# Two products of 256 columns merged into one of 512 in the feed-forward ups of a two-block transformer kernel

## The reference, cut to what matters

```
def causal_dwconv(x, w):            # y[t] = sum_k w[k] x[t-K+1+k], K = 3 here
def conv_ffn(h, w_up, conv_w, w_down):          # FFN 0 and FFN 1: w_up 1024 x 5632
    u = causal_dwconv(h @ w_up, conv_w)
    val, gate = u[..., :D_FF], u[..., D_FF:]    # D_FF = 2816
    return (jax.nn.silu(gate) * val) @ w_down
# FFN 2: w_up 1024 x 4096
    hid = jnp.square(jax.nn.relu(jnp.einsum('bsd,df->bsf', h, w_up[l])))
    x = x + jnp.einsum('bsf,fd->bsd', hid, w_down[l])
```

## Time and profile before

| | us |
|---|---|
| median of 3 runs (all three) | 1196.44 (1191.47, 1196.44, 1197.89) |
| the profiled execution's own time | 1194.65 |
| its span in the trace | 1192.8 |
| PE busy in the span | 1126.8 (94%) |
| DVE, ACT, POOL busy | 545.8, 591.0, 839.5 |
| steady block of FFN 0 and 1 / of FFN 2 | 8.50 / 5.62 |

### The profile page before, as it was taken

How to read it: one execution, slowest core, us unless ns; L and a number is a source line. 1 busy time by engine, 2 the same in 40 slices (tenths; PEclk the granted TensorE clock), 3 DMA queues, 4 the chain that set the end, 5 groups by cost and what they waited for, 6 DMA issues and landing times.

```text
span 1192.8 us, 21692 instructions
## 1 busy us (share of the span) xinstructions
PE 1126.8 (94%) x8119; PEld 1031.3 (86%) x8119; DVE 545.8 (46%) x1122; ACT 591.0 (50%) x894; POOL 839.5 (70%) x303
## 2 busy tenths in 40 slices
PE   5999897999999998999999988999999998999997
PEld 2799797999998987989999968999999987999996
DVE  4568677965657684595232360334111335111112
ACT  0455425454543564455454525455776544545544
POOL 3567458988786534698878747555556777988885
PEclk9899998999999998899999999999999999999999
DMA  9987597999987354497665414544444544656662
GB/s 342 304 270 207 187 290 226 329 329 321 313 296 251 113 142 142 142 313 225 184 187 182 137 57 142 147 137 142 133 151 140 178 159 124 211 178 192 188 181 88
DMA packets 253485, 238.03 MB, mean 200 GB/s; under 512 B 18076, under 2 KB 216529, under 8 KB 253425
## 3 DMA queue, kind: packets, MB, share of 16 engines
q1 hardware_dynamic: 235104, 198.70, 54.1%
q10 hardware_dynamic: 17712, 38.28, 8.8%
q0 software_dynamic: 608, 0.22, 0.1%
HBM read 236.12 MB, written 1.05 MB: 199 GB/s over the span
## 4 chain that ended last, share of the span: by engine, by line
PE 66%; DMA 9%; DVE 8%; ACT 6%; POOL 6%; issue 3%; SPq 0%; ACTq 0%; DVEq 0%; POOLq 0%
PE bank L1270 16%; PE bank L1271 16%; PE bank L1272 16%; POOL unit_lo L726 5%; ACT unit_hi L839 3%; DMA ada<-in_ada_w 2%; PE bank L1295 2%; PE bank L1304 2%; DMA accg<-in_ada_w 2%; PE bank L1296 2%; DMA raw<-in_ev_w_in 2%; DMA raw<-in_ffn_w_up 2%; DVE x L2004 1%; PE bank L1406 1%; PE bank L1331 1%
## 5 line engine op out<-in xcount | busy, mean ns | idle before, releaser
L726 POOL TENSOR_TENSOR unit_lo<-raw,unit_hi 128x2048 fp32r<-128x2048 f32 (+4 forms) x88 | 348.0, 3958 | 228.7 <-ACT unit_hi L839 228.7
L1270 PE MATMUL bank<-h_hi,unit_hi 128*128 128x256 f32 x1152 | 327.1, 284 | 2.9 <-POOL unit_lo L778 2.9
L1271 PE MATMUL bank<-h_lo,unit_hi 128*128 128x256 f32 x1152 | 325.9, 283 | 0.0
L1272 PE MATMUL bank<-h_hi,unit_lo 128*128 128x256 f32 x1152 | 325.9, 283 | 0.0
L778 POOL TENSOR_TENSOR unit_lo<-raw,unit_hi 128x2048 fp32r<-128x2048 f32 (+1 forms) x70 | 257.0, 3672 | 67.8 <-ACT unit_hi L986 66.2
L1270 PEld LDWEIGHTS bank<-h_hi,unit_hi 128*128 128x128 f32 x1152 | 220.7, 192 | 8.7 <-issue 5.9
L1271 PEld LDWEIGHTS bank<-h_lo,unit_hi 128*128 128x128 f32 x1152 | 220.8, 192 | 2.5
L1272 PEld LDWEIGHTS bank<-h_hi,unit_lo 128*128 128x128 f32 x1152 | 220.8, 192 | 0.0
L839 ACT ACTIVATE unit_hi<-raw 128x2048 fp32r<-128x2048 f32 (+4 forms) x98 | 163.1, 1666 | 108.9 <-DMA raw<-in_ffn_w_up 31.4
L781 POOL TENSOR_TENSOR down<-raw_down,down 128x1024 fp32r<-128x1024 f32 x70 | 176.1, 2515 | 0.4 <-ACT down L1012 0.4
L2135 DVE SCALAR_TENSOR_TENSOR work<-bank,cols,work 128x254 f32<-128x254 f32 (+1 forms) x176 | 72.6, 473 | 130.7 <-ACT work L973 130.7
(11 more groups left out here) (355 smaller groups left out, 2197.6 us busy)
## 6 DMA issues: line engine op xcount, KB each, us to landing
raw<-in_ffn_w_up SPq DMA_DIRECT2D x88, 512.0 KB, 5.1
raw<-in_w_in SPq DMA_DIRECT2D x60, 512.0 KB, 4.7
raw_down<-in_ffn_w_down SPq DMA_DIRECT2D x44, 512.0 KB, 4.7
ada<-in_ada_w ACTq DMA_DIRECT2D x16, 1024.0 KB, 6.3
raw<-in_w_up SPq DMA_DIRECT2D x64, 256.0 KB, 3.1
raw_down<-in_w_down SPq DMA_DIRECT2D x32, 512.0 KB, 3.5
raw<-in_ev_w_in SPq DMA_DIRECT2D x28, 512.0 KB, 5.2
att<-in_ada_w ACTq DMA_DIRECT2D x14, 1024.0 KB, 7.0
```

Source lines behind the costliest of these rows:

```text
L726: nc.gpsimd.tensor_tensor(ul[g % 2][:, w], raw[g % 2][:, w], uh[g % 2][:, w].bitcast(F32), ALU.subtract).then_inc(lo_up, 1)
L1270: nc.tensor.matmul(o, sh, mh, start=first, stop=False)
L1271: nc.tensor.matmul(o, sh, ml, start=False, stop=False)
L1272: return nc.tensor.matmul(o, sl, mh, start=False, stop=last)
```

## The change

The two halves of the activations become one tensor `h_both`, in which the low half of a slice lies right of its high half: 512 columns. For blocks 2 and up, high weights by high activations and high weights by low activations are then one matmul of 512 columns, and low by high is one of 256 columns into the left half. A tile fills a whole bank: the left half has high.high + low.high, the right half high.low. The halves must be added on the way out: ACT copies the right half to SBUF (`low_g`, `low_v`), DVE adds it to the left half in the bank (new semaphores `low_out`, `sum_done`).

A block of FFN 0 or 1 now needs two banks: gate in one (`og`), value in the other (`ov`), the same two for every block. The gate is made first. Its bank is waited for by `gate_done(b-1)`, raised by the second gate tap of the block just before; the value's by `bank_free` of the block just before. Both had been one block older. Blocks 0 and 1 of each FFN (`narrow`) are left as they were. FFN 2 keeps a bank per block.

The core of the diff (the first lines put `h_both` in place of `h_hi` and `h_lo`; the ACT part's narrow blocks are as before):

```
@@ tensor part, up
+                    def tile(o, c):
+                        for kt in range(KD):
+                            a = slice(kt * n + c, kt * n + c + P)
+                            nc.tensor.matmul(o[:, :], uh[s][:, a], hb[:, kt, :], start=kt == 0, stop=False)
+                            mm = nc.tensor.matmul(o[:, 0:S], ul[s][:, a], hh[:, kt, :], start=False, stop=kt == KD - 1)
+                        return mm
                     pe.wait_ge(lo_up, b + (g0 + 1))
-                    pe.wait_ge(bank_free[4 + s], i + (g0 + k) // 2)
-                    for j, c in enumerate(range(0, n, P)):
-                        for kt in range(KD):
-                            a, o = slice(kt * n + c, kt * n + c + P), bank[4 + s][:, S * j:S * (j + 1)]
-                            mm = product(o, uh[s][:, a], ul[s][:, a], hh[:, kt, :], hl[:, kt, :], kt == 0, kt == KD - 1)
-                    mm.then_inc(bank_full[4 + s], 1)
+                    if f == 2:
+                        pe.wait_ge(bank_free[4 + s], i + (g0 + k) // 2)
+                        tile(bank[4 + s], 0).then_inc(bank_full[4 + s], 1)
+                        return
+                    og, ov = wide_banks(f)
+                    pe.wait_ge(gate_done, b + act0)
+                    tile(og, P).then_inc(gate_full, 1)
+                    pe.wait_ge(bank_free[5 - s], i + ((g0 + k - 1) // 2 + 1))
+                    tile(ov, 0).then_inc(bank_full[4 + s], 1)
@@ scalar part, FFN 0 and 1, blocks 2 and up
+                        act.wait_ge(gate_full, b + (t0 // 2 - 1))
+                        nc.scalar.activation(low_g, og[:, S:2 * S], ACT.Copy).then_inc(low_out, 1)
+                        act.wait_ge(sum_done, b * 2 + (t0 - 3))
+                        nc.scalar.activation(fg[k], og[:, 0:S], ACT.Copy, scale=scale_g).then_inc(gate_tap, 1)
+                        unit_done()
+                        nc.scalar.activation(low_v, ov[:, S:2 * S], ACT.Copy).then_inc(low_out, 1)
+                        next_high()
+                        act.wait_ge(sum_done, b * 2 + (t0 - 2))
+                        nc.scalar.activation(fv[k], ov[:, 0:S], ACT.Copy, scale=scale_v).then_inc(tap_done, 1)
@@ scalar part, FFN 2
+                        unit_done()
+                        nc.scalar.activation(low_v, bank[4 + s][:, S:2 * S], ACT.Copy).then_inc(low_out, 1)
+                        next_high()
                         act.wait_ge(bank_free[4 + s], i + ((g0 + k) // 2 + 1))
+                        nc.scalar.activation(fv[k], prod, ACT.Relu).then_inc(tap_done, 1)
+                        act.wait_ge(prod_done, b + (act0 - 1))
                         act_high()
@@ vector part (next_modulation issues the next of the four modulation steps; the first waits for ada_in)
+                    if not half and not narrow:
+                        dve.wait_ge(low_out, b + (wide_tiles(2) - 1))
+                        V.tensor_tensor(prod, bank[4 + s][:, 0:S], low_v, ALU.add).then_inc(bank_free[4 + s], 1)
+                    if half and not narrow:
+                        og, ov = wide_banks(f)
+                        t0 = wide_tiles(f)
+                        dve.wait_ge(low_out, b * 2 + (t0 - 3))
+                        V.tensor_tensor(og[:, 0:S], og[:, 0:S], low_g, ALU.add).then_inc(sum_done, 1)
+                        next_modulation()
+                        dve.wait_ge(gate_tap, b + (t0 // 2 - 1))
+                        link(tap(1, 1))
+                        tap(1, 2).then_inc(gate_done, 1)
+                        dve.wait_ge(low_out, b * 2 + (t0 - 2))
+                        V.tensor_tensor(ov[:, 0:S], ov[:, 0:S], low_v, ALU.add).then_inc(sum_done, 1)
+                        next_modulation()
                     dve.wait_ge(tap_done, b + (act0 + 1))
+                    if half and not narrow:
+                        link(tap(0, 1))
+                        tap(0, 2).then_inc(bank_free[4 + s], 1)
...
```

More of the change, by code:

```diff
@@ L343, in build @@
         fg = [work[:, 512 * i + 256:512 * i + 512] for i in range(2)]
+        low_g, low_v = (work[:, 1024 + 256 * i:1280 + 256 * i] for i in range(2))
         acth = [yh[:, i, :] for i in range(2)]
@@ L966, in act_high, with next_high @@
                         nc.scalar.activation(dst, prod, ACT.Copy).then_inc(act_hi, 1)
-                    act.wait_ge(bank_full[4 + s], i + ((g0 + k) // 2 + 1))
+                    last = fixed and b == nb - 1
+                    narrow = fixed and b < 2
+                    def next_high():
+                        if last:
+                            pass
+                        elif fixed:
+                            hi_unit(g0 + b + 2)
+                        else:
+                            act.wait_ge(raw_in[s], i * 32 + (raw_need[g0 + k] + 32))
+                            nc.scalar.activation(uh[s][:, 0:w], raw[s][:, 0:w], ACT.Copy).then_inc(hi_up, 1)
@@ new lines, in body @@
+                    if narrow:
+                        unit_done()
+                        if half:
+                            nc.scalar.activation(fv[k], bank[4 + s][:, 0:256], ACT.Copy, scale=scale_v)
+                            nc.scalar.activation(fg[k], bank[4 + s][:, 256:512], ACT.Copy, scale=scale_g).then_inc(tap_done, 1)
+                        else:
+                            nc.scalar.activation(fv[k], bank[4 + s][:, 0:256], ACT.Relu).then_inc(tap_done, 1)
+                            act.wait_ge(bank_free[4 + s], i + ((g0 + k) // 2 + 1))
+                            act_high()
+                        next_high()
+                    elif half:
+                        og, ov = wide_banks(f)
[9 more added lines that the diff above has]
+                        nc.scalar.activation(fv[k], ov[:, 0:S], ACT.Copy, scale=scale_v).then_inc(tap_done, 1)
+                    else:
+                        unit_done()
+                        nc.scalar.activation(low_v, bank[4 + s][:, S:2 * S], ACT.Copy).then_inc(low_out, 1)
+                        next_high()
@@ L2130, in body @@
                     prod = bank[6][:, S * k:S * (k + 1)]
+                    narrow = isinstance(b, int) and b < 2
                     def tap(j, back):
@@ L2152, in body @@
                         tap(0, 2).then_inc(bank_free[4 + s], 1)
-                        if mod:
-                            dve.wait_ge(ada_in[k], i * 16 + 16 * (mod0 // 2 + 1))
-                            dve.wait_ge(ada_acc, b + mod0)
-                            step = modulation(0)
+                        next_modulation()
+                    if half:
                         dve.wait_ge(silu_done, b + (act0 + 1))
@@ L2159, in body @@
                         V.tensor_tensor(prod, fv[k], prod, ALU.mult).then_inc(prod_done, 1)
-                        if mod:
-                            link.need(step)
-                            step = modulation(1)
+                        next_modulation()
+                    elif narrow:
+                        V.tensor_tensor(prod, bank[4 + s][:, 0:S], fv[k], ALU.mult).then_inc(bank_free[4 + s], 1)
                     else:
-                        V.tensor_tensor(prod, bank[4 + s][:, 0:S], fv[k], ALU.mult).then_inc(bank_free[4 + s], 1)
+                        V.tensor_tensor(prod, prod, fv[k], ALU.mult).then_inc(prod_done, 1)
                     dve.wait_ge(act_hi, b + (act0 + 1))
@@ L2167, in body @@
                     V.tensor_tensor(lo, prod, hi.bitcast(F32), ALU.subtract).then_inc(act_lo, 1)
-                    if mod:
-                        for q in (2, 3):
-                            link.need(step)
-                            step = modulation(q)
+                    for _ in range(3):
+                        next_modulation()
                 per = 2 * (5, 2, 0)[f]
```

48 lines of the change are left out of this document (29 added, 19 removed).

## The result

The changed kernel is slower: 1222.6 us median (1218.96 to 1224.45, six runs) against 1193.74 for the kernel before (1191.47 to 1197.89, six runs beside it), ratio 1.0225, 95% interval 1.0204 to 1.0246. The forecast said slower, 1209, with 1219 as its upper end: right side, wrong size. The profiled execution took 1224.45, its span 1222.6: 29.8 more than the 1192.8 before, where the working of the forecast had +13.3.

The account below looks back on a forecast made before the run. PE was taken as full in all three FFNs. FFN 0 +9.5, FFN 1 +6.4 and FFN 2 -2.6 sum to +13.3 on 1194.65: 1208.0, or 1209.7 against the runs, stated as 1209; range 1198 to 1219.

Parts of the forecast that it names:

- PE saves 0.011 us for each pair, 9.6 in all.: All FFNs: one 512-column matmul replacing two of 256 saves 0.011 us, 9.6 us in all if PE never waits.
- The bounds given, 0 and 19: Limits on PE's total saving in us, as the rows show 512 and 256 columns only apart, never by turns.
- The new wait: FFN 0 and 1: up(b) waits for gate_done(b-1) behind DVE's list; block 7 8.7 us late, block 6 7.6 late respectively.
- The clock falls: Rival, chance 0.05: PE's waits of 2.5 to 3.7 us lower the granted clock twice or thrice; +5 us, 1214.
- The queue shortens as the block lengthens ... I take 8.38.: FFN 0 middle: later-issued pieces queue less, so a block takes 8.38 us; 14 blocks give -1.7 us.
- The loop itself and its 2.5 us: FFN 0 from block 7: landing, step, taps, sum, SiLU, next issue, next landing repeat with period L + 2.5 us.
- L: FFN 0: time from issue to landing of a modulation-weights piece; 6.2 us in the rows, 5.9 enough for 8.4 a block.
- the rival priced (8.7 to 9.5 a block): Loop of the pieces binds FFN 0, chance 0.12: L stays 6.2 or more; +4.5 us, 1213, or +16, 1225.
- The end +2.5.: FFN 0, blocks 20 and 21: two ups without a down between delay the value tile; 2.5 us, in FFN 1 1.4.
- no waits: Rival, chance 0.08: PE waits for neither gate_done nor the piece, only the ends cost; faster, 1190.
- the starts cost half: Rival, chance 0.15: pieces land in 6.2 us and row operations shrink; 8 of 16 us of lateness remain, 1201.

Follow-up runs that it names:

- f1_lo6: Changed kernel with blocks 2 to 5 of FFN 0 and 1 also in the old form, wide from block 6; ratio 1.0159 to the kernel before.
- f3_norow: Probe: changed kernel with DVE's four row operations in each of FFN 0 and 1 cut from 1024 columns to 16; ratio 1.0194 to the kernel before.
- g2_rowp: Probe: changed kernel with DVE's row operations in FFN 0 and 1 cut to 16 columns, second operand read from PSUM; ratio 1.0188 to the kernel before.
- f5_fill: Changed kernel with zero-weight matmuls in PE's waits ahead of blocks 2, 5, 21 of FFN 0 and 2, 5 of FFN 1; ratio 1.0187 to before.
- h1_none: Changed kernel with all blocks of all three FFNs in the old form, only the activations' new layout left; ratio 1.0003 to the kernel before.
- h2_f1mid: Changed kernel with only blocks 6 to 19 of FFN 1 wide, all else in the old form; ratio 1.0002 to the kernel before.
- e2_f2: Changed kernel with only FFN 2 using the 512-column products, FFN 0 and 1 in the old form; ratio 0.9983 to the kernel before.
- e3_f1: Changed kernel with only FFN 1 using the 512-column products, FFN 0 and 2 in the old form; ratio 1.0067 to the kernel before.
- g4_f12: Changed kernel with only blocks 6 to 21 of FFN 1 and FFN 2 wide, FFN 0 in the old form; ratio 1.0010 to the kernel before.
- g1_early: Changed kernel with ACT issuing the next modulation-weights piece behind its scaled gate in wide blocks, before waiting for gate_done and SiLU; ratio 1.0131 to the kernel before.
- e4_end: Changed kernel with blocks 20 and 21 of FFN 0 and 1 in the old form; 1215.6 us, ratio 1.0144 to the kernel before.

## Why the prediction was right or wrong, point by point

**"PE saves 0.011 us for each pair, 9.6 in all."** Mis-sized. Alternating, 512 and 256 columns take 0.3525 together where three of 256 took 0.359: 0.007 a pair, block 8.50 to 8.39, not 8.33. In FFN 2 the up went from 2.88 to 2.82, but the down from 2.74 to 2.78 (1063.42, 1066.20, 1069.02 above). No run shows why the down got longer. All 40 + 30 blocks save 5.3 us, not 9.6. The bounds given, 0 and 19, held it.

**"The new wait": `gate_done(b-1)` behind DVE's list.** Right in kind, and in FFN 1 nearly to the number. FFN 1, moved by the 19.9 us that it begins later: up(2) at 516.1 (forecast 516.0), up(3) at 526.6 (525.7), up(4) at 536.2 (536.2), up(5) at 548.6 (548.2). FFN 0, moved by 2.2: up(2) 206.5 (206.45), up(7) ends at 262.3 (262.9). There the end is met with some luck: up(4), up(5) and up(6) started 2.1 to 2.4 us earlier than forecast, and then came a wait of 1.34 ahead of block 7 that the forecast did not have. f1_lo6 shows that in FFN 1 these waits, with the slow tiles behind them, are the whole excess. But what I put down as DVE's time in the row operations is in good part a wait for POOL (f3_norow, g2_rowp).

**"The clock falls", chance 0.05, +5 us.** It fell at five waits: ahead of blocks 2, 11 and 21 of FFN 0 and 2 and 5 of FFN 1; the tiles behind them took 7.23, 7.23, 8.24, 7.23 and 8.28 us instead of 5.64, 10 us together. f5_fill, with PE kept at work ahead of four of these five, got back about 4.5. FFN 1's start missed by 2.9 us, and its steps show where. The 1.6 us that block 2's tile lost were taken out of the waits ahead of blocks 3 and 4 (0.42 and 0.95 instead of 1.2 and 2.1), so up(4) and up(5) started as forecast; block 5's 2.6 had no wait behind it to go into and came on top. My argument against it (2.5 to 3.7 us "are far shorter" than the idle stretch in the earlier trace rows) took one row for the limit; no row showed that shorter waits are harmless.

**"The queue shortens as the block lengthens ... I take 8.38."** This is the step that failed: +6.5 instead of -1.7, half of the whole miss. The loop itself and its 2.5 us were right (2.6 measured); L did not fall to 5.9 but was 6.3 on the mean and uneven, 5.3 one way and 7.0 the other. With 2.6 that is a round of 8.9, and PE's blocks took 9.0. I had the rival priced (8.7 to 9.5 a block) and gave it 0.12 for a hope that nothing in the rows supported. Even the 6.2 was one execution's value: with FFN 0 in the old form the median for `ada` in 290:356 is 6.2 in three profiles (before, h1_none, h2_f1mid) and 7.0 to 7.2 in three others (e2_f2, e3_f1, g4_f12), and any of these puts the loop above PE's block. g1_early shows the cause: same order, same transfers, earlier issue, and the loss in the middle is gone.

**"The end +2.5."** 5.9: late landing and a wait of 3.67, then a tile at half clock (2.6). e4_end got it back; g1_early most of it. In FFN 1, without pieces, it was 0.5 where I said 1.4.

**Not slower, "no waits" (0.08) and "the starts cost half" (0.15).** Both refuted: the starts cost 18.6 us together. "The starts cost half" was priced on the row operations shrinking; in g2_rowp they did, to 0.17 us, and the starts still cost 11.7.

Sum of the misses: FFN 0 middle 8.2, its end 3.4, its start -0.7; FFN 1 2.9 + 1.1 - 0.9; FFN 2 1.7; the rest 0.6. Together 16.3, which but for rounding is the 29.8 less 13.3.

## What to carry to other kernels

When a change puts a wait for a transfer ahead of something that the next issue of that transfer depends on, it closes a loop; work out its period with the durations that the trace shows, the slow ones too, and do not let the queue get shorter on credit. Look first for the edit that opens the loop: here one DMA issue moved ahead of one wait was worth 11 us. And a saving of 1.3% of a block (0.11 of 8.50) does not pay for a block of slack where DVE or a transfer already runs late: it showed in the profile only where they did not, in FFN 1 from block 6 on and in FFN 2.
